# Six page slots that hold keys first, key scores around the first heads, and a new split of the sorting

## The reference, cut to what matters

```python
def dsa_sample(q, k, v, qi, ki, wi, ck, cv, cki, page_table):
    ...
    isc = indexer_scores(qi, ki_all, wi)              # which tokens matter
    isc = jnp.where(adm[None], isc, -jnp.inf)
    vals, sel = lax.top_k(isc, topk)                  # 256 of 1028
    ...
    kg = jnp.where(is_past, ck[phys, off].astype(k.dtype), gather_rows(k, new_i))
    vg = jnp.where(is_past, cv[phys, off].astype(v.dtype), gather_rows(v, new_i))
    return sparse_attend(q, kg, vg, jnp.isfinite(vals))

def sparse_attend(q, kg, vg, valid):
    logits = jnp.einsum('bqhd,bqkhd->bqhk', q.astype(F32), kg.astype(F32)) * DH_A ** -0.5
    logits = jnp.where(valid[:, :, None, :], logits, -jnp.inf)
    p = jax.nn.softmax(logits, axis=-1)
    return jnp.einsum('bqhk,bqkhd->bqhd', p, vg.astype(F32))
```

## Time and profile before

| | us |
|---|---|
| median of 3 runs | 1445.48 |
| the three runs | 1446.64, 1445.48, 1438.57 |
| profiled execution, its time | 1446.08 |
| profiled execution, its span | 1444.3 |
| PE busy in the span | 1398.7 |
| DVE busy in the span | 1057.4 |

### The profile page before, as it was taken

One profiled execution on the slowest core, in us unless ns is written; L12 is line 12 of the kernel. 1 busy time (PEld: TensorE's weight loads), 2 busy tenths in 40 slices (PEclk: granted clock), 3 DMA queues, 4 the chain that ended last, 5 costly groups with the idle time before them and its releaser, 6 DMA issues.

```text
span 1444.3 us, 28367 instructions
## 1 busy us (share of the span) xinstructions
PE 1398.7 (97%) x11508; PEld 1288.7 (89%) x11508; DVE 1057.4 (73%) x1366; ACT 349.4 (24%) x670; POOL 353.8 (24%) x300
## 2 busy tenths in 40 slices
PE   9999999999988988999999999999999999999997
PEld 9999999996343987999999999999996669999996
DVE  6977686768877546797768697768677676887764
ACT  5111102002453434421110221110202455221100
POOL 0533212005400023453311253311200002543310
PEclk9999999999898999999999999999999879999998
DMA  8443542665787104644355344354261305444152
GB/s 324 169 155 113 193 164 89 223 218 171 272 292 284 55 3 179 226 152 169 116 186 201 139 157 164 117 189 169 89 215 65 145 34 226 174 152 170 53 171 79
DMA packets 63202, 233.40 MB, mean 162 GB/s; under 512 B 9019, under 2 KB 18816, under 8 KB 46204
## 3 DMA queue, kind: packets, MB, share of 16 engines
q1 hardware_dynamic: 50970, 224.82, 44.2%
q10 hardware_dynamic: 11554, 6.37, 1.5%
q0 software_dynamic: 576, 0.74, 0.2%
HBM read 225.67 MB, written 6.10 MB: 160 GB/s over the span
## 4 chain that ended last, share of the span: by engine, by line
PE 55%; DVE 2%; ACT 1%; DMA 1%; issue 1%; POOL 1%; DVEq 0%; ACTq 0%; POOLq 0%
PE psum L193 16%; PE psum L195 16%; PE psum L194 15%; PE psum L262 1%; PE psum L267 1%; PE psum L263 1%; DMA ring<-in_w_gu 1%; PE psum L393 0%; POOL ysq_ab_out L3097 0%; PE psum L389 0%; PE psum L386 0%; DMA ring<-in_w_cd 0%; PE psum L2942 0%; PE psum L2891 0%; PE psum L2822 0%
## 5 line engine op out<-in xcount | busy, mean ns | idle before, releaser
L193 PE MATMUL psum<-x_hi_r,pair_hi 128*128 128x288 f32 x1736 | 514.7, 296 | 3.0 <-PEq L123 2.2
L195 PE MATMUL psum<-x_hi_r,ring_r 128*128 128x288 f32 x1736 | 514.5, 296 | 0.0
L194 PE MATMUL psum<-x_lo_r,pair_hi 128*128 128x288 f32 x1608 | 474.8, 295 | 0.0
L188 DVE TENSOR_TENSOR ring_r<-ring,pair_hi 128x2048 fp32r<-128x2048 f32 (+1 forms) x129 | 336.2, 2608 | 26.8 <-ACT pair_hi L183 23.0
L193 PEld LDWEIGHTS psum<-x_hi_r,pair_hi 128*128 128x128 f32 x1736 | 328.1, 189 | 4.4 <-issue 3.2
L195 PEld LDWEIGHTS psum<-x_hi_r,ring_r 128*128 128x128 f32 x1736 | 327.7, 189 | 0.0
L194 PEld LDWEIGHTS psum<-x_lo_r,pair_hi 128*128 128x128 f32 x1608 | 303.5, 189 | 0.0
L193 PE MATMUL psum<-hidden_hi_r,down_hi 128*128 128x288 f32 x704 | 208.4, 296 | 0.0
L194 PE MATMUL psum<-hidden_r,down_hi 128*128 128x288 f32 x704 | 207.7, 295 | 0.0
L195 PE MATMUL psum<-hidden_hi_r,down_r 128*128 128x288 f32 x704 | 207.0, 294 | 0.0
L744 POOL TENSOR_TENSOR hidden<-silu,up 128x288 f32 x88 | 126.5, 1438 | 147.9 <-ACT silu L662 145.3
(11 more groups left out here) (562 smaller groups left out, 1866.6 us busy)
## 6 DMA issues: line engine op xcount, KB each, us to landing
ring<-in_w_gu SPq DMA_DIRECT2D x87, 1024.0 KB, 4.9
down<-in_w_down SPq DMA_DIRECT2D x64, 704.0 KB, 4.2
ring<-in_w_ab SPq DMA_DIRECT2D x18, 1024.0 KB, 5.2
ring<-in_w_cd SPq DMA_DIRECT2D x12, 1024.0 KB, 5.9
ring<-in_cache_k SPq DMA_DIRECT2D x32, 256.0 KB, 4.5
index_keys<-in_cache_k SPq DMA_DIRECT2D x32, 256.0 KB, 5.7
index_keys<-in_cache_i ACTq DMA_DIRECT2D x64, 64.0 KB, 2.7
eight_pages_ds<-in_cache_v SPq DMA_DIRECT2D x16, 256.0 KB, 6.6
```

Source lines behind the costliest of these rows:

```text
L188: return eng.tensor_tensor(lo, a, hi.bitcast(F32), ALU.subtract)
L193: pe.matmul(out, w_hi, x_hi, start=start, stop=False)
L194: pe.matmul(out, w_hi, x_lo, start=False, stop=False)
L195: return pe.matmul(out, w_lo, x_hi, start=False, stop=stop)
```

## The change

All six slots hold keys first: `KEY_SLOTS` gives sequences 0 to 5 a slot each, and 6 and 7 reuse slots 0 and 1. Values follow in freed slots: 0 and 1 in slots 5 and 2, 2 and 3 in slots 0 and 1, 4 and 5 in 3 and 4, 6 and 7 in 5 and 2. `key_scores` is cut by chunk: group 0's first chunk stands ahead of head 0, its other two behind head 0's scores; group 1's first chunk stands behind values(1) at head 3, its other two behind values(2) at head 4. Slot 4's keys are read in two pieces each. `keys_out(0)` on ACT moves from behind head 7 to behind head 1. Because the numbers of sequences are now needed for keys and, much later, again for values, SP reads them a second time: 64 more reads, put between the page loads. `STEPS` deals the sorting out anew; from head 5 on it is as before.

```diff
-STEPS = (4, 8, 20, 29, 32, 35, SORTED + 2, SORTED + 5, SORTED + 9)
+STEPS = (4, 12, 17, 21, 28, 35, SORTED + 2, SORTED + 5, SORTED + 9)
...
+KEY_BANKS = ((6, 7, 5), (5, 6, 7))
...
-        KEY_SLOTS = (0, 1, 2, 3, 0, 1, 2, 3)
-        KEY_LOADS = (1, 1, 1, 1, 2, 2, 2, 2)
-        VALUE_SLOTS = (4, 5, 0, 1, 2, 3, 4, 5)
-        VALUE_LOADS = (1, 1, 3, 3, 3, 3, 2, 2)
+        KEY_SLOTS = (0, 5, 2, 1, 4, 3, 0, 1)
+        KEY_LOADS = (1, 1, 1, 1, 1, 1, 2, 2)
+        VALUE_SLOTS = (5, 2, 0, 1, 3, 4, 5, 2)
+        VALUE_LOADS = (2, 2, 3, 3, 2, 2)
+        HALF_LANDED = (2, 5)
...
             for u in range(2):
                 sp.wait_ge(S["kv_used"], 2 + 2 * u)
-                for b in range(4, 8):
+                for b in (6, 7):
                     load("cache_k", b, KEY_SLOTS[b], range(4 * u, 4 * u + 4))
+                idx.read_numbers(sp, c, u)
+            for b in (0, 1):
+                load("cache_v", b, VALUE_SLOTS[b])
+            idx.read_numbers(sp, c, 2, 3)
             for u in range(2):
                 sp.wait_ge(S["kv_used"], 6 + 2 * u)
                 for b in (2, 3):
                     load("cache_v", b, VALUE_SLOTS[b], range(4 * u, 4 * u + 4))
+            idx.read_numbers(sp, c, 4, 5)
             for b in (4, 5):
                 load("cache_v", b, VALUE_SLOTS[b])
+            idx.read_numbers(sp, c, 6, 7)
             rk.rows_load(sp)
...
-            def key_scores(g):
+            def key_scores(g, ch):
...
+                if g == 1 and ch == 0:
+                    pe.wait_ge(S["ks_out"], 3)
+                if ch == 0:
+                    for b in four:
+                        pe.wait_ge(kv_landed[KEY_SLOTS[b]], 128 * KEY_LOADS[b])
...
+            key_scores(0, 0)
             for h in range(8):
...
-                if h == 2:
-                    key_scores(0)
+                if h == 0:
+                    key_scores(0, 1)
+                    key_scores(0, 2)
+                if h == 3:
+                    key_scores(1, 0)
+                if h == 4:
+                    key_scores(1, 1)
+                    key_scores(1, 2)
             probs_out(7)
             values(6)
             values(7)
             rk.decay_products(pe)
-            key_scores(1)
-
+            rk.decays_taken(pe)
+            rk.rate_products(pe)
+            rk.rates_taken(pe)
             pe.wait_ge(S["ms_done"], 1)
```

More of the change, by code:

```diff
@@ L1689, in page_of, with key_parts, by_page @@
             return two_pages[:, (j - 6) * 512:(j - 5) * 512] if j >= 6 else spare[:, PIECES[j]:PIECES[j] + 512]
+        def key_parts(slot, ch):
+            def by_page(a):
+                return a.rearrange("p (j h n) -> p j h n", h=HP, n=P)
+            if slot == 5:
+                return [(0, 512, by_page(eight_pages[:, 4 * ch:4 * ch + 4].rearrange("p j n -> p (j n)")))]
+            if slot < 4:
+                return [(0, 512, by_page(slots[slot][:, 2048 * ch:2048 * ch + 2048]))]
+            if ch == 0:
+                return [(0, 384, by_page(spare[:, PIECES[0]:PIECES[2] + 512])), (384, 128, by_page(spare[:, PIECES[3]:PIECES[3] + 512]))]
+            return [(0, 256, by_page(spare[:, PIECES[4]:PIECES[5] + 512])), (256, 256, by_page(two_pages[:, :]))]
         B = c.banks
@@ L1709, in load_halves @@
                     for e in range(2):
-                        load(src, b + e, slots_of[b + e], range(4 * u, 4 * u + 4), 4 + u)
+                        load(src, b + e, slots_of[b + e], range(4 * u, 4 * u + 4), HALF_LANDED[u])
             send_pair_loop(c, sp, stream, RING, 3)
@@ L1731, in sync @@
             sp.wait_ge(c.pair_done, first + npairs + 2)
-            load("cache_k", 1, KEY_SLOTS[1])
+            load("cache_k", 3, KEY_SLOTS[3])
             rk.mask_load(sp)
@@ L1735, in sync @@
                 sp.wait_ge(S["is_sum"], 3 * u + 2)
-                load("cache_k", 2 + u // 2, KEY_SLOTS[2 + u // 2], range(4 * (u % 2), 4 * (u % 2) + 4))
+                b = 2 if u < 2 else 5
+                load("cache_k", b, KEY_SLOTS[b], range(4 * (u % 2), 4 * (u % 2) + 4))
             sp.wait_ge(S["is_used"], 12)
-            load("cache_v", 0, VALUE_SLOTS[0], range(3))
+            load("cache_k", 4, KEY_SLOTS[4], range(3))
             idx.read_numbers(sp, c, 6, 7)
@@ L1871, in values @@
                 mm.then_inc(S["op_sum"], 1)
-            def key_scores(g):
-                if g == 0:
+            def key_scores(g, ch):
+                four = range(4 * g, 4 * g + 4)
+                c0, w = CHUNKS[ch]
+                if g == 0 and ch == 0:
                     pe.wait_ge(v_done, 3)
                     pe.wait_ge(S["qz_done"], 1)
+                if g == 0 and ch == 2:
                     pe.wait_ge(S["is_out"], 2)
-                else:
[L1880 to L1896, removed]
@@ new lines, in key_scores @@
+                if g == 1 and ch == 0:
+                    pe.wait_ge(S["ks_out"], 3)
+                if ch == 0:
+                    for b in four:
+                        pe.wait_ge(kv_landed[KEY_SLOTS[b]], 128 * KEY_LOADS[b])
+                out = B[KEY_BANKS[g][ch]]
+                for h in range(HP):
+                    for b in four:
+                        parts = [(o, n, a[:, :, h]) for o, n, a in key_parts(KEY_SLOTS[b], ch)] if ch < 2 else [(0, w, k[:, h, TP:NT])]
+                        for o, n, rhs in parts:
+                            mm = pe.matmul(out[32 * (b % 4):32 * (b % 4) + 32, o:o + n], qz[:, b, h], rhs, start=(h == 0 and o == 0), stop=(g == 0 and h == HP - 1),
+                                           skip_group_check=(g == 1))
@@ L1898, in tensor @@
+                if ch < 2:
+                    mm.then_inc(S["kv_used"], 2)
+                else:
+                    mm.then_inc(S["ks_sum"], 4)
+            key_scores(0, 0)
             for h in range(8):
```

19 lines of the change are left out of this document (10 added, 9 removed).

## The result

The changed kernel takes 1463.23 us (median of 4 runs, 1460.55 to 1466.01); the kernel before, run beside it, 1443.14 (4 runs, 1438.57 to 1446.64). The ratio is 1.0152, 95% interval 1.0130 to 1.0174: slower by 1.3% to 1.7%. The profiled execution took 1465.27 us, with a span of 1463.5, which is 19.2 us more than before. The forecast was 1465, in a range of 1453 to 1472.

A forecast was written before the change was run, and what follows sets the result against it. PE was taken as the bound, busy 1398.7 of 1444.3 us; a mask 15.8 us later plus 3.2 us of half clock gave 19 us on 1446.08, so 1465 us after 0.6 for the median, range 1453 to 1472.

The forecast's parts named there:

- Step 1: Loop start to head 3: PE starts near 378.3 and reaches key_scores(1,0) at about 398, at no cost of its own.
- Step 2: Keys 6 and 7, loaded in halves around eight SP reads, land at 406.9; PE waits there some 9 us.
- Step 3: Last keys' landing to head 5: about 7 us of half clock, 0.5 us for slot 4's pieces; head 5 at 420.9.
- Step 4: Head 5 to mask: 23.5 us as before, mask ready at 444.4 and spread at once, 15.8 us later.
- Step 5: Mask spreading: PE idles some 5 us ahead, then spreads at half clock in 7.3 to 8 us, adding 3.2 us.
- Step 6: SP's late work: key_norms' table issued at about 460, values 0 to 3 early; all hidden by the mask's delay, otherwise not.
- the rival with the keys in time: Keys 6 and 7 cause no stall; mask 2.9 us later, clock 3.2, table some 2: about +9, 1455; chance 0.14.

The follow-up runs named there:

- experiment 6: Changed kernel with SP's table reads dealt anew, none between page loads PE waits for, 32 more reads than before instead of 64; 1452.92 us, ratio 1.0080.
- experiment 1: Changed kernel with the eight table reads between the two halves of keys 6 and 7 moved behind the second half; 1458.70 us, ratio 1.0116.
- experiment 3: Kernel before with eight table reads added on SP between the two halves of the loads of keys 4 to 7; 1446.13 us, ratio 1.0035.
- experiment 4: Changed kernel with all of key_scores(1) put back behind decay_products, SP's queue as changed; 1462.33 us, ratio 1.0139.
- experiment 5: Changed kernel with the sorting split STEPS as in the kernel before; 1460.25 us, ratio 1.0151.
- experiment 10: Six slots with SP dealt anew, but key scores, copy and sorting where the kernel before has them; 1446.98 us, ratio 1.0041.
- experiment 11: Experiment 10 with the 16 re-reads of sequences 0 and 1 moved ahead of the loads of keys 6 and 7; 1442.51 us, ratio 1.0003.
- experiment 7: Experiment 6 with keys_out(0) on ACT behind head 2 instead of head 1; 1456.28 us, ratio 1.0092.
- experiment 8: Experiment 6 with key_scores(1) put back behind decay_products and keys_out(0) moved behind head 3; 1447.28 us, ratio 1.0036.
- experiment 9: Experiment 6 with the last two chunks of the second key scores moved from behind head 4 to behind the rate products; 1450.02 us, ratio 1.0065.
- experiment 12: Experiment 11 with the first chunk of the first key scores moved from behind head 2 to behind head 1's scores; 1440.92 us, ratio 0.9994.
- experiment 2: Experiment 1 with the table reads of sequences 6 and 7 also moved, from ahead of the stores into an earlier gap; 1458.58 us, ratio 1.0107.

## Why the prediction was right

**Step 1, the start of the loop.** Up to the wait for ACT the work went as costed, and the wait was 1.96 us, forecast "some 2". What the step left out is the half clock behind this wait: from the start of its first key scores to the wait for the last keys PE took 399.2 - 376.65 = 22.5 us, where the step had 398 - 378.3 = 19.7. The end, 397.64 + 1.54 = 399.2, came near the forecast only because the stage began earlier. In the changed kernel this error hid in the stall behind it; experiment 6 uncovered it.

**Step 2, the last keys.** SP was through with their issues at 389.45 + 13.27 = 402.72, forecast 402.3 to 402.7; the keys released PE at 407.88, forecast 406.9; the wait was 8.7 us, forecast 9. The median landing was 4.2 us and the longest 5.3; from SP's last issue to PE's release it was 407.88 - 402.72 = 5.2, so here the slowest page counted and not the median one, and that is the missing microsecond. Experiments 1, 3 and 6 show the cause from three sides. They also show what the step had too simple: it added reads, issues and landing, but without the 4.4 us of reads between them the wait fell by 3.0 only, 0.9 of the difference because the last page then took longer to land (experiment 1). Of the two figures for the landing, the median of the row (4.5) was nearer than the 2.6 us that the prediction estimated from the Trainium skill, "DMA: Bandwidth & Descriptors", section on the anatomy of one DMA; that page's fit is for transfers issued by GpSimd, and these are issued by SP. The fastest page again agrees with it (2.7). The same page's floor of about 600 ns for a tensor_load, in its section on latency, was the rule that spoke against the change, and the trace agrees roughly, with 0.553 us per read: 16 reads filled 8.85 us before, and the holes between SP's batches here are as wide.

**Step 3, from the landing to head 5.** The step had the stall bring the clock down; it was down since 391.55. Behind the stall half clock lasted 3.7 us, not 7, so the first chunk took 413.30 - 407.88 = 5.4 us, not 6.8; and the pieces of slot 4 cost nothing, where 0.5 was added: the two last chunks took 420.01 - 416.12 = 3.89 us against 3.87 before. Head 5 started at 420.01, forecast 420.9; one late and two early microseconds.

**Step 4, head 5 to the mask.** 443.37 + 0.18 - 420.01 = 23.54 us, forecast 23.5. The step held exactly on DVE. Its second half, that PE would stand ready, did not quite: PE was let go 0.2 us after the mask, by ACT's rates.

**Step 5, the clock at the mask.** The spreading took 447.64 + 4.02 - 443.78 = 7.9 us, forecast 7.3 to 8, against 4.1 before, and 3.3 us of that reached key_norms, forecast 3.2. The size was right and the reason was not: the prediction had PE idle 5 us ahead of the mask, but PE had been at half clock since 431.6, its decay and rate products took 4.2 us each instead of 2.17, and it arrived just in time, with 0.59 us of idling.

**Step 6, SP's tail.** The table for key_norms was issued at 460.96, forecast about 460, and no one waited for it. That it "would not be hidden without" the delay is what experiment 4 shows: 7.8 us for the table and 4.3 for values 6 and 7, where the rival with the keys in time had priced 2 us and the experiment's expectation 5 to 10.

**The sum** was 15.8 + 3.2 = 19; by the same points it measured 15.1 + 3.3 = 18.4 at key_norms, and 19.2 at the end, after other stretches of clock that add 2.7 and take back about 2. Within the stage, the 1.7 us of an earlier start made up for a mask that was 1 us later than costed. So the wait, its cause and its size to a microsecond are the prediction's merit; that the total came within 2 us is also luck, with errors of 1 to 3 us that cancelled and a rest of the program that differs by 6 us between profiles.

Two sums of the prediction are slightly off, without effect on the forecast. The two ends in step 2 are 404.2 and 411.4 by its own terms, not 403.9 and 411.2. The first rival's terms add up to 2.9 + 3.2 + 2 = 8.1 us and 1453.6, not 9 and 1455.

Shown by experiment: SP's reads are about half of the loss (6); the split of the sorting adds nothing while the keys are late (5); slots and transfers are none of it once the reads are hidden (10, 11). The other half is PE's new order with ACT's copy behind head 1 and the new split, shown as one: experiment 10 takes the three back with SP's queue as in 6 (ratios 1.0080 and 1.0041, although its values come 6.9 us late), and 11 then hides the last reads (1.0003). How it divides between order, copy, split and clock stays open: 7, 8 and 9 each moved a piece, and each got another stall of 1.3 to 2.4 us and, in 8 and 9, another long stretch at the lower level in exchange.

## What to carry to other kernels

A register that is read from a table costs the queue's engine real time in program order (0.55 us each here); before pages are dealt to slots in a new way, count the reads that the new order needs and lay them into holes of that queue, because the buffers were free here and the reads were not. When a stall is expected, look at what it hides on the other queues, since removing it alone may win next to nothing (experiment 4). And where three engines take turns, a piece of work moved into one's queue comes out as waits of the others: four orders tried here (7, 8, 9, 12) each bought off one stall and got another.

## What the runs showed of the hardware

That the lower clock can outlast the idling by far was not expected. Behind a wait of only 1.81 us, PE ran from 434.2 to 451.6 at 0.50 while it was busy 16.22 of 17.40 us, and came back to the 2.4 GHz level only from about 459.4. In experiment 8 it was 0.50 for 15 us with PE busy 14.18 of them, behind a wait of 2.25. In the kernel before, the two stretches behind idle time ended within some 7 to 8 us; and in experiment 11 a wait of the same 1.81 us (at 413.54) was followed by decay products at full clock (2.18 us). The runs don't show what decides it.

Key scores in pieces of 128, 256 and 384 columns cost nearly the same as in one piece of 512, in time of PE at full clock: 421.23 - 417.62 = 3.61 us for the chunk with pieces of 384 and 128 in experiment 10, before 422.64 - 419.07 = 3.57; and 3.89 for the chunk with pieces of 256 and the small one, before 3.87. Each large chunk has 8 more instructions.

The time from issue to landing was no constant. For the same 16 key pages of the ring the medians were 4.2 to 4.6 us with eight reads between the halves (as changed, experiments 4 and 5), 4.6 to 5.4 without reads between them (1, 10, 11, 12), and 6.3 to 7.8 where in addition SP had issued the page loads ahead of them less than 6 us before (2, 6, 7, 8, 9). So reads between loads cost less than their own time: in experiment 1 the last page landed 0.9 us sooner behind its issue with them than without.
